# A two-block transformer forward pass on one core: GpSimd's modulation sums, the places of their tiles, shift and scale as rows, and the order of the memory attention

## The chip, the cores and the metric

One core of one Trainium2 chip runs the whole computation in one launch. The metric is the time of the device in microseconds. Three runs of the kernel before gave 1160.01, 1160.11 and 1162.4 us; the median is 1160.11 us. All data is float32.

## The reference

`first_block` takes x (256 tokens, width 1024), a context of 256 tokens and a vector c. Cut to what matters here:

```
sh1, sc1, g1, sh2, sc2, g2 = split(silu(c) @ w_ada + b_ada, 6)      # 1024 each
hc = rmsnorm(ctx) * (1 + csc1) + csh1 ;  hl = rmsnorm(x) * (1 + sc1) + sh1
# gated linear attention (4 heads) and retention (4 heads) of hl, with states from hc
x = x + g1 * merge(gla, ret)
x = x + g2 * hier_moe(rmsnorm(x) * (1 + sc2) + sh2)                  # 32 experts, top 2
```

`second_block` then adds a sparse attention mixer, an attention over 256 memory tokens (4 heads of 128: softmax(q k / sqrt(128)) v, then w_xo), and a feed-forward of width 4096 with squared relu.

## The kernel before, in words

Every weight matrix is cut into tiles of 1 MB ([128, 2048]) that lie in DRAM in the order of their use, the stream. SP loads them into a ring of six slots, `ring`; four of TensorE's results at a time lie in PSUM banks 0 to 3. `plan()` writes both orders out by hand: `SUMS` is the order of TensorE's results, each a name such as `rv1.3` or `gate4`, and `FREED` says for each tile of the stream which event frees its slot. SP's `load(t)` waits for the event of tile t-6 and issues the load, strictly in the order of the stream. A result is announced by `sum_ready`, and `fresh(name)` on TensorE waits, by `sum_taken`, until the result four places earlier has been copied out. The readers (ScalarE or VectorE) must take the results in the order of `SUMS`.

The projections of the mixer are `folded` products of a pair of tiles: seven block products with sums of the weights that VectorE forms in place (`weights_fold`, L2341 to L2348), after which `blocks_summed` (L2375 to L2402) puts the blocks together. The order is `gk`, `gv0`, `gv1`, four products `e`, `rk`, `rv0`, `rv1`, `rq`, then eight states `sg`, `sr`, and then eight rounds of gates: `fac0` to `fac7` with `gate0` to `gate7`. In the first four rounds ScalarE makes exponentials (`decays`), VectorE multiplies them with q and k (`gla_factors`, L2468 to L2474), and TensorE forms the scores from them (L1667).

The modulation (sh2, sc2, g1, g2) does not run on TensorE as a whole: 16 tiles of w_ada, called ada tiles, go through the same ring, and `ADA_BEHIND` says how many stand behind which pair or gate. GpSimd's `tile_weighted` multiplies the eight 256-column pieces of such a tile with one silu(c) per partition (L697) and adds the pieces up in three steps of 1024, 512 and 256 columns (L699 to L703). What is left is a sum over the 128 partitions. For tiles 0 to 7 (sh2 and sc2) TensorE does it in `columns_summed` (L1506) after `rq`: 16 products of a 128x128 block with a column of ones, so that the result lies in columns of 8, and ScalarE copies it to `mod2` (L907). The sums 0 to 7 lie where `qdec`, a table of decays, is loaded later; sums 8 to 11 lie over `rkc`, which is free once `ctxk_ready` has come to 8; tiles 12 to 15 wait for `fac3`. Broadcast rows of small parameters, `rows`, are loaded by GpSimd's queue ahead of its first tile (L686).

The memory attention (`query_exps`, `query_turned` on ScalarE, `query_weighted`, `out_copied` on VectorE): for each of four heads ScalarE forms the exponentials of the scores (L1330), VectorE divides them by their sum (L3182), TensorE transposes them (L2147), ScalarE copies the transposed ones out (L1340), TensorE multiplies them with v (L2156), and VectorE copies the result out (L3188). TensorE runs the transposes of head n ahead of the product of head n-1. Then it goes on with w_xo (L2168).

The diff touches `plan`, `program` with its blocks for the engines (the nested `tile_weighted`, `columns_summed`, `query_exps` and `query_turned` are in it), and `stream_of`.

## Time and profile before

| | us |
|---|---|
| median of three runs | 1160.11 |
| profiled execution | 1161.98 |
| its span, first to last instruction | 1160.2 |
| TensorE busy in it | 1118.5 |
| VectorE busy | 567.3 |
| ScalarE busy | 304.9 |
| GpSimd busy | 190.7 |

PE is TensorE's matmuls, DVE VectorE, ACT ScalarE, POOL GpSimd, SP the queue that issues the loads. In a timeline each row has the start and the length in us, the engine and the line of the kernel, the operation with its output and input by name, their shapes, and how many instructions are merged (x); in brackets how long the engine was idle before, and what ended that.
### The profile page before, as it was taken

To read this page: it belongs to the slowest core of one execution; us is meant where nothing else is said; L and a number is where in the kernel's file an instruction comes from. 1 tells how busy PE (TensorE), PEld (TensorE's weight loads), DVE (VectorE), ACT (ScalarE), POOL (GpSimd) and SP (SyncE) were. 2 spreads that over 40 slices of the span, in tenths; PEclk is the share of its full clock that TensorE was granted. 3 is DMA by queue.
4 is the path that set the end of the run, shared out by engine and by line. 5 is a ranking of instruction groups with operands and counts; after the bars stand their busy time and mean duration, and the time that the engine had idled before them with its cause. 6 is when DMAs were issued, how large, how long until landed. Compare 5 with 4: busy or idle time off the path is not lost.

```text
span 1160.2 us, 16672 instructions
## 1 busy us (share of the span) xinstructions
PE 1118.5 (96%) x6704; PEld 842.0 (73%) x6704; DVE 567.3 (49%) x1161; ACT 304.9 (26%) x708; POOL 190.7 (16%) x219
## 2 busy tenths in 40 slices
PE   7999999999999999999999999999888989999998
PEld 6789888898887888885555554478666849997443
DVE  1345345423676585532222222238886435677555
ACT  4360010015412302151111110253574241321000
POOL 0053665644670020000000000010000000000000
PEclk9999999999999999999999999999989989999999
DMA  9952232453444444568999999833300413544541
GB/s 377 392 214 109 109 146 109 166 233 145 146 167 159 178 150 183 197 255 335 423 426 425 426 425 425 363 123 133 122 1 20 180 55 110 185 179 182 182 145 38
DMA packets 35020, 241.92 MB, mean 209 GB/s; under 512 B 3978, under 2 KB 4234, under 8 KB 6524
## 3 DMA queue, kind: packets, MB, share of 16 engines
q1 hardware_dynamic: 33500, 234.46, 51.9%
q0 software_dynamic: 864, 4.16, 0.9%
q10 hardware_dynamic: 576, 2.18, 0.5%
q8 instruction: 56, 0.92, 0.3%
q14 instruction: 24, 0.20, 0.0%
HBM read 239.74 MB, written 1.05 MB: 208 GB/s over the span
## 4 chain that ended last, share of the span: by engine, by line
PE 85%; DVE 6%; ACT 3%; DMA 2%; issue 2%; SPq 1%; DVEq 0%; ACTq 0%
PE bank L1440 20%; PE bank L1437 11%; PE bank L1836 10%; PE bank L2191 8%; PE bank L1417 7%; PE bank L1863 5%; PE bank L1488 4%; PE bank L1793 3%; PE bank L1800 2%; DMA arena<-in_stream 2%; PE bank L1408 2%; PE bank L1639 1%; PE bank L2168 1%; PE bank L1693 1%; PE bank L1696 1%
## 5 line engine op out<-in xcount | busy, mean ns | idle before, releaser
L1440 PE MATMUL bank<-ring,arena 128*128 128x256 f32 x784 | 174.2, 379 | 1.6 <-ACT arena L1260 0.7
L1440 PEld LDWEIGHTS bank<-ring,arena 128*128 128x128 f32 x784 | 148.0, 190 | 22.3 <-ACT arena L1260 1.0
L697 POOL TENSOR_SCALAR ring<-ring,sc,consts 128x256 f32<-128x256 f32 x128 | 89.9, 716 | 108.2 <-DMA ring<-in_stream 83.5
L868 ACT ACTIVATE arena<-bank 128x256 f32<-128x256 f32 x90 | 32.4, 381 | 193.9 <-PE bank L1440 158.3
L1417 PE MATMUL bank<-ring,arena 128*128 128x256 f32 x320 | 71.0, 380 | 0.0
L1417 PEld LDWEIGHTS bank<-ring,arena 128*128 128x128 f32 x320 | 60.3, 190 | 9.3 <-issue 0.8
L1437 PE MATMUL bank<-arena,ring 128*128 128x128 f32 x528 | 63.0, 275 | 0.0
L1437 PEld LDWEIGHTS bank<-arena,ring 128*128 128x128 f32 x528 | 61.7, 192 | 0.5
L1836 PE MATMUL bank<-ring,arena 128*64 128x256 f32 x512 | 57.0, 381 | 0.0
L1417 PE MATMUL bank<-ring,hTl 128*128 128x256 f32 x256 | 56.6, 379 | 0.0
L1417 PEld LDWEIGHTS bank<-ring,hTl 128*128 128x128 f32 x256 | 48.3, 190 | 8.1 <-issue 1.9
L1836 PEld LDWEIGHTS bank<-ring,arena 128*64 128x64 f32 x512 | 36.0, 137 | 24.1 <-issue 6.7
L1488 PE MATMUL bank<-ring,arena 128*128 128x256 f32 x224 | 51.8, 386 | 1.7 <-ACT arena L766 0.8
L2776 DVE TENSOR_TENSOR arena<-arena,bank 128x256 f32<-128x256 f32 x16 | 6.7, 422 | 93.6 <-ACT arena L1082 93.6
L1437 PE MATMUL bank<-memkv,ring 128*128 128x128 f32 x448 | 52.3, 275 | 0.0
L1437 PEld LDWEIGHTS bank<-memkv,ring 128*128 128x128 f32 x448 | 51.2, 192 | 0.0
L2341 DVE TENSOR_TENSOR ring<-ring 128x1024 f32<-128x1024 f32 x24 | 29.6, 1235 | 43.2 <-PE bank L1440 32.8
L1488 PEld LDWEIGHTS bank<-ring,arena 128*128 128x128 f32 x224 | 42.5, 193 | 8.9 <-ACT arena L766 1.0
L1082 ACT ACTIVATE arena<-bank 128x256 f32<-128x256 f32 x16 | 6.1, 383 | 157.0 <-PE bank L1836 157.0
L741 POOL TENSOR_SCALAR arena<-arena,rA 128x1024 f32<-128x1024 f32 x2 | 5.7, 2830 | 252.7 <-ACT arena L1034 252.7
L1440 PE MATMUL bank<-ring,hTl 128*128 128x256 f32 x192 | 45.6, 380 | 0.0
L766 ACT ACTIVATE arena<-bank 128x512 f32<-128x512 f32 x38 | 22.2, 604 | 87.7 <-PE bank L1417 26.5
(514 smaller groups left out, 2012.5 us busy)
## 6 DMA issues: line engine op xcount, KB each, us to landing
ring<-in_stream SPq DMA_DIRECT2D x163, 1024.0 KB, 7.2
arena<-in_stream SPq DMA_DIRECT2D x38, 1024.0 KB, 13.4
hTl<-in_stream SPq DMA_DIRECT2D x9, 1024.0 KB, 11.7
hTc<-in_stream SPq DMA_DIRECT2D x9, 1024.0 KB, 13.6
consts<-in_consts ACTq DMA_DIRECT2D x1, 1408.0 KB, 12.9
arena<-in_mem SPq DMA_DIRECT2D x2, 512.0 KB, 5.2
arena<-in_x SPq DMA_DIRECT2D x1, 1024.0 KB, 18.8
arena<-in_ctx SPq DMA_DIRECT2D x1, 1024.0 KB, 23.4
```

Of the source, the lines that this page charges most:

```text
L697: pool.tensor_scalar(wk, wk, scv[:, k, 0:1], ones[:, 0:1], ALU.mult, ALU.mult).then_inc(ada_step, 1)
L868: ins = act.activation((p[:, 0, :], p[:, 1, :], first)[n], b, ACT.Copy)
L1408: mm = pe.matmul(b[:, 256 * n:256 * n + 256], w[:, k, 128 * n:128 * n + 128], h[:, k, :], start=(k == 0), stop=(k == KD - 1))
L1417: mm = pe.matmul(b[:, 256 * i:256 * i + 256], h[:, k, 128 * i:128 * i + 128], w[:, k, :], start=(k == 0), stop=(k == KD - 1))
L1437: mm = pe.matmul(b[:, 128 * n:128 * n + 128], rhs[:, k, 128 * n:128 * n + 128], lhs(*source, k), start=(start and k == 0 and n == 0), stop ...
L1440: mm = pe.matmul(b, lhs(*source, k), rhs[:, k, :], start=(start and k == 0), stop=(k == 3), skip_group_check=True)
L1488: mm = pe.matmul(b[:, 256 * i:256 * i + 256], h[:, k, 128 * i:128 * i + 128], w[:, k, :], start=(k == 0 and i == 0), stop=(k == KD - 1), s ...
L1793: mm = pe.matmul(gather_bank(o, k)[:, 256 * j:256 * j + 256], xn2[:, j, 128 * k:128 * k + 128], Pm[:, j, :], start=True, stop=True)
L1836: mm = pe.matmul(bank[0][CAP * e:CAP * e + CAP, FF * a:FF * a + FF], rows_k[:, at:at + CAP], w[e][:, k, :], start=(k == 0), stop=(k == KD ...
L1863: mm = pe.matmul(bank[1 + m][to:to + CT, :], hT_PT[n % 2][:, of:of + CT], wd[e][:, k, 512 * m:512 * m + 512], start=(k == 0), stop=(k == 1 ...
L2191: mm = pe.matmul(prod[m][:, :], lhs, rhs, start=(q == 0), stop=(q == 15))
L2341: dve.tensor_tensor(b11, b12, b11, ALU.subtract).then_inc(weights_folded, 1)
```

## The change

It has five parts. GpSimd adds the eight pieces of a tile in seven additions of 256 columns, each waiting for the one before. The ada tiles stand at other places of the stream: behind gk, gv0, gv1, rk, rv0, rv1, rq and gates 0 to 7 there were 1, 1, 2, 1, 2, 1, 1 and 1, 1, 1, 1, 1, 1, 1, 0 tiles, and now there are 1, 2, 2, 2, 2, 2, 1 and 0, 1, 1, 1, 1, 0, 0, 0. Shift and scale are summed as rows: a column of ones is the stationary operand, the sums of a tile are the 256 moving columns, and the four tiles of `sh` go to output partitions 0, 32, 64 and 96 of one bank, those of `sc` likewise, between `rv1` and `rq`; VectorE copies the eight rows into `rows`, which was cleared before, TensorE transposes them after `rq` into a new result, `mod2`, and ScalarE takes every 32nd column of it. The broadcast that fills `rows` is issued after that. GpSimd runs tiles 8 to 11 before it waits for the modulation and loads `qdec`. In the memory attention ScalarE makes the exponentials of all four heads first, and VectorE copies out the transposed ones of head 0 in its place.

```diff
@@ -143,9 +143,10 @@
 
 
 
-ADA_STEPS = KD + 3
+ADA_STEPS = KD + 7
 TURNS = (4, 5, 7, 8, 2, 0, 1, 3)
-ADA_BEHIND = {"gk": 1, "gv0": 1, "gv1": 2, "rk": 1, "rv0": 2, "rv1": 1, "rq": 1, "gate": 1}
+ADA_BEHIND = {"gk": 1, "gv0": 2, "gv1": 2, "rk": 2, "rv0": 2, "rv1": 2, "rq": 1, "gate": (0, 1, 1, 1, 1, 0, 0, 0)}
+ROWS_BEHIND = {"rv1": ("sh", "sc"), "rq": ("mod2",)}
 
 
 def plan():
@@ -191,16 +192,16 @@
     for name in ("rk", "rv0", "rv1", "rq"):
         pair(name)
         ada(ADA_BEHIND[name])
-    sums.extend(["sh", "sc"])
+        sums.extend(ROWS_BEHIND.get(name, ()))
     sums.extend(f"sg{h}" for h in range(HEADS))
     sums.extend(f"sr{h}" for h in range(HEADS))
     sums.append("fac0")
     tile("gate0")
-    ada(1)
+    ada(ADA_BEHIND["gate"][0])
     for i in range(7):
         sums.append(f"fac{i + 1}")
         tile(f"gate{i + 1}")
-        ada(ADA_BEHIND["gate"] * (i < 6))
+        ada(ADA_BEHIND["gate"][i + 1])
 
     pair("mg0")
     sums.extend(["g1a", "g1b"])
@@ -683,7 +684,8 @@
             pool.wait_ge(adaT_ready, 2)
             pool.dma_start(wr[:, :], wr_d).then_inc(small_in, 16)
             pool.dma_start(wukv[:, :], wukv_d).then_inc(small_in, 16)
-            pool.dma_start(rows[:, :], rowdram.partition_broadcast(P)).then_inc(rows_in, 16)
+            pool.wait_ge(cleared, 2)
+            pool.memset(rows[:, 0:2 * TC], 0.0).then_inc(cleared, 1)
             scv = sc[:, :].rearrange("p (k c) -> p k c", c=2)
             ada_at = [t for t, (kind, _) in enumerate(FREED) if kind == "ada"]
 
@@ -695,24 +697,27 @@
                 for k in range(KD):
                     wk = w[:, TC * k:TC * k + TC]
                     pool.tensor_scalar(wk, wk, scv[:, k, 0:1], ones[:, 0:1], ALU.mult, ALU.mult).then_inc(ada_step, 1)
-                pool.wait_ge(ada_step, ADA_STEPS * n + KD)
-                pool.tensor_tensor(w[:, 0:1024], w[:, 0:1024], w[:, 1024:2048], ALU.add).then_inc(ada_step, 1)
-                pool.wait_ge(ada_step, ADA_STEPS * n + KD + 1)
-                pool.tensor_tensor(w[:, 0:512], w[:, 0:512], w[:, 512:1024], ALU.add).then_inc(ada_step, 1)
-                pool.wait_ge(ada_step, ADA_STEPS * n + KD + 2)
-                pool.tensor_tensor(ada_sum(n), w[:, 0:256], w[:, 256:512], ALU.add).then_inc(ada_step, 1)
-
-            pool.wait_ge(cleared, 2)
+                wk = w.rearrange("p (k n) -> p k n", k=KD)
+                for k in range(4):
+                    pool.wait_ge(ada_step, ADA_STEPS * n + KD + k)
+                    pool.tensor_tensor(wk[:, k, :], wk[:, k, :], wk[:, k + 4, :], ALU.add).then_inc(ada_step, 1)
+                for k in range(2):
+                    pool.wait_ge(ada_step, ADA_STEPS * n + KD + k + 4)
+                    pool.tensor_tensor(wk[:, k, :], wk[:, k, :], wk[:, k + 2, :], ALU.add).then_inc(ada_step, 1)
+                pool.wait_ge(ada_step, ADA_STEPS * n + KD + 6)
+                pool.tensor_tensor(ada_sum(n), wk[:, 0, :], wk[:, 1, :], ALU.add).then_inc(ada_step, 1)
+
+            pool.wait_ge(cleared, 3)
             pool.wait_ge(sc_ready, 2)
             pool.wait_ge(consts_in, 32)
             for n in range(8):
                 tile_weighted(n)
             pool.wait_ge(ctxk_ready, 8)
-            tile_weighted(8)
-            pool.wait_ge(sum_ready, NO["sc"] + 1)
+            for n in range(8, 12):
+                tile_weighted(n)
+            pool.wait_ge(sum_ready, NO["mod2"] + 1)
             pool.dma_start(C("qdec"), cdram[:, where["qdec"][0]:where["kdec"][0]]).then_inc(qdec_in, 16)
-            for n in range(9, 12):
-                tile_weighted(n)
+            pool.dma_start(rows[:, :], rowdram.partition_broadcast(P)).then_inc(rows_in, 16)
             pool.wait_ge(sum_ready, NO["fac3"] + 1)
             for n in range(12, 16):
                 tile_weighted(n)
@@ -899,13 +904,17 @@
             folded("rk", [parts_l, parts_c], [head_block(rqk[:, :, 1, :])(0, 0), rkc[:, 0, 0:256]])
             for p in range(2):
                 folded(f"rv{p}", [parts_l, parts_c], [v[:, 0, 512 * p:512 * p + 256] for v in (rv, rvc)])
+            for _ in ("sh", "sc"):
+                taken.one()
             folded("rq", [parts_l], [head_block(rqk[:, :, 0, :])(0, 0)])
             act.wait_ge(sum_taken, taken.n)
-            act.wait_ge(sum_taken, NO["sh"])
-            for q, name in enumerate(("sh", "sc")):
-                b = take(name)
-                act.activation(mod2[:, KD * q:KD * q + KD], b[:, 0:KD], ACT.Copy).then_inc(sum_taken, 1)
-                taken.one()
+            b = take("mod2")
+            src = b[:, :].rearrange("p (s n g r) -> p s g n r", s=2, n=2, g=4)[:, :, :, :, 0]
+            dst = mod2[:, :].rearrange("p (s g n) -> p s g n", s=2, g=4)
+            for q in range(2):
+                act.activation(dst[:, q, :, :], src[:, q, :, :], ACT.Copy).then_inc((act_step, sum_taken)[q], 1)
+            step.one()
+            taken.one()
             for h in range(HEADS):
                 copy(f"sg{h}", sg[:, h, :, :])
             for h in range(HEADS):
@@ -1339,14 +1348,11 @@
                     act.wait_ge(av_done, 2 * STEPS + m - 1)
                 act.activation(xPT[m % 2], bank[(NO["xp00"] + 2 + m % 2) % NB][:, :], ACT.Copy).then_inc(pt_taken, 1)
 
-            query_exps(0)
-            query_exps(1)
-            query_turned(0)
-            query_exps(2)
-            query_turned(1)
-            query_exps(3)
-            query_turned(2)
-            query_turned(3)
+            for n in range(XH):
+                query_exps(n)
+            act.wait_ge(pt_taken, 2 * STEPS + 4 + 1)
+            for m in range(1, XH):
+                query_turned(m)
             preload(ACT.Sqrt)
             act.wait_ge(ox_ready, 4)
             preload(ACT.Sqrt)
@@ -1498,13 +1504,22 @@
                 return mm
 
             pe.wait_ge(tables_in, 16)
-            def columns_summed(name, at):
+            def shifts_summed(name, at):
 
                 b = fresh(name)
                 pe.wait_ge(ada_step, ADA_STEPS * (at + 4))
-                for k in range(KD):
-                    mm = pe.matmul(b[:, k:k + 1], ada_sum(at + k // 2)[:, 128 * (k % 2):128 * (k % 2) + 128], ones[:, 0:1],
+                for g in range(4):
+                    mm = pe.matmul(b[32 * g:32 * g + 1, 0:TC], ones[:, 0:1], ada_sum(at + g),
                                    start=True, stop=True, skip_group_check=True)
+                mm.then_inc(sum_ready, 1)
+
+            def shifts_turned():
+
+                pe.wait_ge(cleared, 3)
+                pe.wait_ge(sum_taken, NO["sc"] + 1)
+                b = fresh("mod2")
+                for blk in range(4):
+                    mm = pe.transpose(b[:, 128 * blk:128 * blk + 128], rows[:, 128 * blk:128 * blk + 128], ident)
                 mm.then_inc(sum_ready, 1)
 
             def rows_summed(name, at):
@@ -1626,10 +1641,11 @@
             for p in range(2):
                 folded(f"rv{p}", tile(), tile(), [latents, context])
                 pool_tiles(ADA_BEHIND[f"rv{p}"])
+            shifts_summed("sh", 0)
+            shifts_summed("sc", 4)
             folded("rq", tile(), tile(), [latents], features=True)
             pool_tiles(ADA_BEHIND["rq"])
-            columns_summed("sh", 0)
-            columns_summed("sc", 4)
+            shifts_turned()
             for name, kd, v, n in (("sg", kd_g, gvc, 4), ("sr", kd_r, rvc, 8)):
                 pe.wait_ge(ctxk_ready, n)
                 for h in range(HEADS):
@@ -1656,7 +1672,7 @@
 
             before_factors(0)
             token_rows("gate0", tile(), hl)
-            pool_tiles(ADA_BEHIND["gate"])
+            pool_tiles(ADA_BEHIND["gate"][0])
             for i in range(8):
                 f = fac[i % 2]
                 pe.wait_ge(factors, i + 1)
@@ -1682,7 +1698,7 @@
                 if i < 7:
                     before_factors(i + 1)
                     token_rows(f"gate{i + 1}", tile(), hl)
-                    pool_tiles(ADA_BEHIND["gate"] * (i < 6))
+                    pool_tiles(ADA_BEHIND["gate"][i + 1])
                 pe.wait_ge(scores_taken, i + 1)
                 if i >= 2:
                     pe.wait_ge(values_taken, i - 1)
@@ -2457,6 +2473,16 @@
                                       ALU.mult).then_inc(ctxk_ready, 1)
             for p in range(2):
                 folded(f"rv{p}", ring_tiles(PAIR_AT[f"rv{p}"]), [parts_l, parts_c], [block_of(rv, 512 * p), block_of(rvc, 512 * p)])
+            dve.wait_ge(cleared, 3)
+            for q, name in enumerate(("sh", "sc")):
+                dve.wait_ge(sum_taken, NO[name])
+                dve.wait_ge(sum_ready, NO[name] + 1)
+                for g in range(4):
+                    ins = dve.tensor_copy(rows[32 * g:32 * g + 1, TC * q:TC * q + TC], bank[NO[name] % NB][32 * g:32 * g + 1, 0:TC])
+                    if g < 3:
+                        S(ins)
+                        step.one()
+                ins.then_inc(sum_taken, 1)
             folded("rq", ring_tiles(PAIR_AT["rq"]), [parts_l], [head_block(rqk[:, :, 0, :])])
 
             def gla_factors(h):
@@ -3203,10 +3229,12 @@
             max_scaled(3)
             query_weighted(0)
             query_weighted(1)
+            dve.wait_ge(pt_ready, 2 * STEPS + 4 + 1)
+            dve.tensor_copy(xPT[0], bank[(NO["xp00"] + 2) % NB][:, :]).then_inc(pt_taken, 1)
+            query_weighted(2)
             out_copied(0)
-            query_weighted(2)
+            query_weighted(3)
             out_copied(1)
-            query_weighted(3)
             out_copied(2)
             out_copied(3)
             dve.wait_ge(sum_taken, NO["xp00"])
@@ -3328,7 +3356,7 @@
         s += [column_tile(win, at + 256 * j) for j in range(2)] + ada_tiles(ADA_BEHIND[name] if name else 0)
     gate_tiles = [column_tile(win, gga + 256 * i if i < 4 else rga + 256 * (i - 4)) for i in range(8)]
     for i in range(8):
-        s += [gate_tiles[i]] + ada_tiles(ADA_BEHIND["gate"] * (i < 7))
+        s += [gate_tiles[i]] + ada_tiles(ADA_BEHIND["gate"][i])
     for p in range(2):
         for w, at in ((win, mga), (win, mga + 1024), (a["w_branch_gla"][0], 0), (a["w_branch_ret"][0], 0)):
             s += [column_tile(w, at + 512 * p + 256 * j) for j in range(2)]
```

## Rows read from the trace of the kernel before

**Rows 1.** The page, part 1: busy time, share of the span, instructions.

```profile
PE 1118.5 (96%) x6704; PEld 842.0 (73%) x6704; DVE 567.3 (49%) x1161; ACT 304.9 (26%) x708; POOL 190.7 (16%) x219
```

**Rows 2.** Timeline of PE, 180 to 345 us: start, length, operation, idle before.

```profile
204.71 1.89 PE L1440 MATMUL bank<-ring,hTl 128*128 128x256 f32 x8
...
227.15 1.89 PE L1440 MATMUL bank<-ring,hTc 128*128 128x256 f32 x8
...
230.04 2.02 PE L1437 MATMUL bank<-hTl,ring 128*128 128x128 f32 x16 [1.00 <-DVE arena L2394]
...
242.62 3.63 PE L1506 MATMUL bank<-consts 128*128 128x1 f32 x32
...
246.12 15.75 PE L1639 MATMUL bank<-arena 128*128 128x256 f32 x64
...
271.18 0.49 PE L1667 MATMUL bank<-arena 128*128 128x128 f32 x2 [1.09 <-DVE arena L2474]
...
311.37 0.49 PE L1667 MATMUL bank<-arena 128*128 128x128 f32 x2 [0.90 <-DVE arena L2474]
...
325.75 7.07 PE L1417 MATMUL bank<-ring,hTl 128*128 128x256 f32 x32
```

**Rows 3.** Windows: busy time of each engine, PEclk (granted clock), DMA share.

```profile
240.00:256.00 16.00, 16.00 (x95) 14.51 (x95) 1.41 (x4) 2.74 (x6) 9.16 (x12) 0.89 0.66 263
...
930.00:945.00 15.00, 10.51 (x38) 6.64 (x38) 5.95 (x20) 8.32 (x23) 0.00 (x0) 0.77 0.00 1
```

**Rows 4.** Timeline of POOL, GpSimd's modulation tiles.

```profile
209.76 7.16 POOL L697 TENSOR_SCALAR ring<-ring,sc,consts 128x256 f32<-128x256 f32 x8 [12.44 <-DMA ring<-in_stream]
...
225.86 2.35 POOL L699 TENSOR_TENSOR ring<-ring 128x1024 f32<-128x1024 f32 x1
...
264.21 0.73 POOL L703 TENSOR_TENSOR arena<-ring 128x256 f32<-128x256 f32 x1
...
300.22 4.30 POOL L697 TENSOR_SCALAR ring<-ring,sc,consts 128x256 f32<-128x256 f32 x8 [24.65 <-PE bank L1652]
...
304.60 2.35 POOL L699 TENSOR_TENSOR ring<-ring 128x1024 f32<-128x1024 f32 x1
...
308.70 1.05 POOL L703 TENSOR_TENSOR arena<-ring 128x256 f32<-128x256 f32 x1
```

**Rows 5.** Timeline of DVE, 195 to 312 us.

```profile
202.25 0.76 DVE L2394 TENSOR_TENSOR arena<-arena 128x256 f32<-128x256 f32 x2
...
226.42 3.48 DVE L2394 TENSOR_TENSOR arena<-arena 128x256 f32<-128x256 f32 x2
...
267.56 2.27 DVE L2468 TENSOR_TENSOR arena<-arena 128x512 f32<-128x512 f32 x3 [24.31 <-ACT arena L944]
...
279.76 1.90 DVE L2468 TENSOR_TENSOR arena<-arena 128x512 f32<-128x512 f32 x3 [5.72 <-ACT arena L944]
...
305.78 4.53 DVE L2468 TENSOR_TENSOR arena<-arena 128x512 f32<-128x512 f32 x3 [5.03 <-ACT arena L944]
```

**Rows 6.** Timeline of PE, 30 to 62 us.

```profile
40.19 3.66 PE L1542 MATMUL bank<-arena 128*32 128x256 f32 x64 [0.51 <-DMA arena<-in_stream]
```

**Rows 7.** Timeline of all engines, 920 to 952 us, memory attention.

```profile
932.29 1.61 PE L2147 MATMUL bank<-consts,arena 128*128 128x128 f32 x8 [1.88 <-DVE arena L3182]
...
932.98 0.60 ACT L1340 ACTIVATE arena<-bank 128x512 f32<-128x512 f32 x1 [0.81 <-PE bank L2147]
...
933.47 0.56 ACT L1330 ACTIVATE arena<-bank,smx,qfac 128x256 f32<-128x256 f32 x1
...
935.74 0.43 DVE L3188 COPY arena<-bank 128x256 f32<-128x256 f32 x1 [2.72 <-PE bank L2156]
...
936.95 1.11 PE L2147 MATMUL bank<-consts,arena 128*128 128x128 f32 x4 [1.24 <-DVE arena L3182]
...
941.01 0.66 PE L2147 MATMUL bank<-consts,arena 128*128 128x128 f32 x4 [1.24 <-DVE arena L3182]
...
943.38 9.18 PE L2168 MATMUL bank<-ring,arena 128*128 128x512 f32 x21
```

## The prediction

> **What bounds the kernel now.** I read the page first: TensorE is busy 96% of the span, VectorE 49%, ScalarE 26%, GpSimd 16% [rows 1]. So a cut on another engine is worth only what TensorE waits for it, and the 42 us in which TensorE is not busy are most of what can be won by waiting less. Second, the timeline of TensorE: around the change it waits three times, 1.00 us before `rq` (at 229.0), 1.09 us at 270.1 and 0.90 us at 310.5, each time for VectorE [rows 2]. Third, the windows with the granted clock: a busy TensorE also loses time where its clock is at the lower of its two levels (1.2 instead of 2.4 GHz). Mean 0.89 over 240 to 256 us is 3.5 us at half speed (16 x 0.11 x 2), which costs 1.75 us; mean 0.77 over 930 to 945 is 6.9 us at half speed [rows 3]. These five places are what the change can touch; everything else should shift as it is.
>
> The times below are of the profiled execution, 1161.98 us with a span of 1160.2; it is 1.9 us above the median of 1160.11, so I subtract the sum from the median.
>
> **GpSimd's sums in pieces.** Before, a tile has 8 products and adds of 1024, 512 and 256 columns. A VectorE addition with two SBUF operands that starts under one of these adds is held until it ends, and then the two engines take turns: L2394, twice 0.4 us normally, took 3.48 us [rows 5] while the 2.35 us add ran from 225.86 [rows 4]; L2468's three took 4.53 us from 305.78, against 1.90 us undisturbed [rows 5], beside the adds begun at 304.60. Under the products the price is small: 2.27 us at 267.56 [rows 4, 5]. The Trainium skill ("SBUF — State Buffer", Who interferes with whom) has the rule: a VectorE instruction with two SBUF inputs and a GpSimd one that reads SBUF exclude each other for the whole instruction. The trace agrees; it also says that VectorE's new copies out of PSUM, one input each, stay free.
>
> The cost: seven pieces of 0.73 us [rows 4] with 0.08 us between are 5.7 us, against 4.5 for three adds (304.60 less the gaps): 1.1 us more per tile, 16 times, on an engine that is 16% busy. The gain for VectorE is not simply the ratio of lengths. A short chain wins: two additions wait at most two pieces. A long chain loses, because it meets one piece per instruction. At 305.78 seven VectorE instructions follow one another (three L2468, four small). I lay the pieces out from 304.60: the first addition waits until 306.14, the next two and the four small ones wait behind a piece each (0.73, stretched to 1.05 like the one at 308.70 where a long VectorE instruction goes first), and the last ends at 311.7 instead of 311.3. So the wait of 0.90 us grows by **0.4 us**. Bounds: -0.9 (the wait goes) to +1.5.
>
> **Places in the stream.** Tiles 0 to 11 now all lie ahead of the gates, so GpSimd is done with tile 11 at about 246 instead of 275, and the factors at 267.56 run undisturbed: 0.37 us on L2468, 0.3 us on the small ones behind. The wait at 270.1 falls from 1.09 to 0.44: **-0.65 us** (bounds -0.9 and 0).
> What it could cost is a late weight tile. Pairs take 24.2 us (204.7 to 228.9, [rows 2]); two tiles of GpSimd behind a pair take about 2 x 12 = 24 us, one landing 5 us after the slot falls free (209.76, [rows 4]). The ring's next pair needs those slots a whole pair later, so some 12 us of slack are left. The slimmest place is `gate5`: SP issues it behind tile 15's load, which waits for tile 12, and tile 12 waits for `fac3`. From 300.22 [rows 4] tile 12 takes 11 us, the two loads 8 us more: 319.3, while `gate5` is needed at 325.75 [rows 2]. 6.5 us of slack, no cost. The broadcast of `rows` leaves GpSimd's queue at 47 us and returns at about 246 beside `qdec`; their readers come 60 us later and more. Nothing. The memset of `rows` ends before tile 0 lands: nothing.
>
> **Shift and scale as rows.** Removed: 16 matmuls with one moving column, 3.5 us from 242.62 to 246.12. The low clock of this stretch lies right behind them: the 64 matmuls begun at 246.12 took 15.75 us, where the 0.216 us per record of its neighbours (eight in 1.89 less the tail) give 13.8 [rows 2, 3]. Added, before `rq`: two times four matmuls with one stationary column into four groups of 32 output partitions. The matmuls of L1542, which also go to four such groups, run side by side: 64 records in 3.66 us, 0.46 us for four logical products [rows 6]. I take 0.45 us for `sh` and for `sc`; one after the other they would be 1.73 us each (0.216 per record, [rows 2]). Added, after `rq`: four transposes, at most the 0.66 us of [rows 7], as a stream 0.45.
> A new wait comes with it. TensorE's first product of `rq` needs the bank of `sh`, which VectorE frees after its last two additions of `rv1` (done at 229.9) and four copies, each 0.35 to 0.43 us long [rows 7]: 231.4, TensorE goes on at 231.55 against 230.04 before. In that gap lie the 0.9 us of row sums and the old wait of 1.00, whose cause (L2394) now only touches GpSimd's products or small pieces. VectorE's copies for `sc` then end at 232.9, just before `rq`'s first part is ready at 233.3, so ScalarE and the weight folds behind them wait for nothing new. `rq` keeps its 12.6 us (244.15), the transposes end at 244.6, L1639 starts then instead of at 246.12: **-1.5 us** (bounds: -2.6, if the wait is nil; -0.3, if the row sums run one after another).
> The low clock behind 246.12 should not come, as the 3.5 us of one-column matmuls ahead of it are gone: **-1.7 us** (bounds: -1.75; 0, if the new idle time and one-row matmuls at 229 to 231.5 bring a fall of their own).
>
> **Memory attention.** Before, ScalarE has one order for exponentials and copies, so heads 2 and 3 start only at 933.47, after the copy that waited for the transposes (932.98) [rows 7]. TensorE then waits 1.24 us twice for VectorE's scaling, which in turn stands behind `out_copied` [rows 7]. After, ScalarE goes through all eight exponentials (a head is 1.1 us: done by 934.3), VectorE takes head 0's copy (0.7 us), scaling of head 2 is done at 934.55 instead of 936.9, of head 3 by about 936.1 instead of 941.0. TensorE has 4 x (0.45 + 0.86) us of work at the full clock from 932.29. Laid out event by event, with the clock low for 3.5 us from head 1's transposes on, as long as behind 246.12, and not for the 6.9 us of before [rows 3], the last product ends and L2168 starts at 939.7 instead of 943.38: **-3.7 us**. With a full clock throughout it would be 938.4 (-5.0), with the clock low as long as before 941.4 (-2.0). The 1.88 us wait ahead of 932.29 [rows 7] stays: nothing in front of it changes.
>
> **Sum.** 0.4 - 0.65 - 1.5 - 1.7 - 3.7 = -7.15 us: 1160.11 - 7.15 = **1153.0 us**.
>
> **The rivals.** (a) The clock falls where it did not: at 229 to 231.5 TensorE now idles 1.6 us beside 0.9 us of one-row matmuls. For it: before 932.29 an idle time of 1.88 us was followed by a fall. Against it: the 1.00 us at 229 was not. 3.5 us more at the lower level cost 1.7: 1154.7. (b) The low clock in the memory attention lasts its 6.9 us again, 1154.7: half of the instructions there are transposes. For it: it stayed low before although TensorE had work of both kinds there (the four transposes at 936.95 took 1.11 us, those at 941.01 0.66); against it: the idle gaps between the heads go [rows 3, 7]. The Trainium skill ("TensorE: Matmul & The Clock Gate", Part 4: PE-mode transpose) states that transposes do not count as activity for the clock; no run here isolates that. (c) Only one of the two halves pays, for instance because the row sums are serial and the new VectorE copies are slower: 1157.5 to 1158.5. (d) Slower: GpSimd becomes the bound of the ring. If taking turns with VectorE stretches all pieces and products, so that a tile takes 22 us at 300, `gate5` lands 4 us late, `gate6` another 7, and the sum is +4: 1164.3. It decides from 17.5 us per tile; for it speaks only that the longest tile before took 12 us and each gets 1.1 more; against it the 6.5 us of slack. (e) No fall of the clock at all in the memory attention: 1151.7.
>
> **How the numbers follow.** My forecast 50% (own range 1151 to 1155.5), (a) 12%, (b) 12%, (c) 12%, (d) 5%, (e) 9%. The range 1150 to 1158.3 holds all but (d), a part of (c) and a remainder for what I did not see. Under 0.2% (2.3 us) cannot be told from no change in this kernel: faster is below 1157.8. Faster 0.84, same 0.10, slower 0.06.
>
> **What would show it.** Right: PEclk 1.00 in 240 to 256; row-sum matmuls of 0.45 us per four; TensorE idle about 1.6 us ahead of `rq`, 0.4 at 270 and 1.3 at 310 (shifted by the gains before); L2168 3 to 5 us closer behind the first transposes of the attention; no wait of TensorE for a DMA of `ring`. Wrong: a DMA wait at a gate, a granted clock of half at 231, a tile of GpSimd over 17 us, or the waits at 270 and 310 unchanged.

## The result, and the profile after

The kernel after took 1154.94 us in the median (20 executions, 1152.3 to 1158.15), the kernel before beside it 1160.76 us (1157.8 to 1168.65). The ratio is 0.9937, 95% interval 0.992 to 0.9953: 0.6% faster. I had predicted 1153.0, range 1150 to 1158.3. The profiled execution took 1155.67 us with a span of 1153.9, against 1160.2 before; all differences below are of these two unless another is named. The page, part 1, of the kernel after:

```profile
PE 1114.2 (97%) x6692; PEld 838.0 (73%) x6692; DVE 564.5 (49%) x1170; ACT 304.2 (26%) x707; POOL 208.2 (18%) x284
```

GpSimd works 17.5 us more (16 tiles by 1.1) and nobody waits for it. TensorE around the change, timeline after, against [rows 2]:

```profile
229.68 1.04 PE L1512 MATMUL bank<-consts 128*1 128x256 f32 x16
...
232.55 2.02 PE L1443 MATMUL bank<-hTl,ring 128*128 128x128 f32 x16 [1.83 <-DVE rows L2481]
...
245.12 0.60 PE L1522 MATMUL bank<-consts,rows 128*128 128x128 f32 x4
...
245.56 13.98 PE L1655 MATMUL bank<-arena 128*128 128x256 f32 x64
...
268.00 0.49 PE L1683 MATMUL bank<-arena 128*128 128x128 f32 x2 [0.24 <-DVE arena L2500]
...
307.69 0.49 PE L1683 MATMUL bank<-arena 128*128 128x128 f32 x2 [0.40 <-DVE arena L2500]
```

Read from the top: all 16 records of the row sums in 1.04 us, so the four column groups run side by side; the wait ahead of `rq` at 1.83 us, where it was 1.00, now for VectorE's copies; the 64 products of the states in 13.98 us, where they took 15.75; the two waits for the gate factors at 0.24 and 0.40 us, where they were 1.09 and 0.90. VectorE's side of it, against [rows 5]:

```profile
227.12 1.55 DVE L2410 TENSOR_TENSOR arena<-arena 128x256 f32<-128x256 f32 x2
...
230.62 3.58 DVE L2481 COPY rows<-bank 1x256 f32<-1x256 f32 x8
...
265.24 1.90 DVE L2494 TENSOR_TENSOR arena<-arena 128x512 f32<-128x512 f32 x3 [19.49 <-ACT arena L953]
...
302.60 3.16 DVE L2494 TENSOR_TENSOR arena<-arena 128x512 f32<-128x512 f32 x3 [5.03 <-ACT arena L953]
305.69 0.81 DVE L2498 TENSOR_TENSOR arena<-arena 128x128 f32<-128x128 f32 x1
306.42 0.28 DVE L2500 TENSOR_TENSOR arena<-arena 128x128 f32<-128x128 f32 x1
306.63 0.81 DVE L2498 TENSOR_TENSOR arena<-arena 128x128 f32<-128x128 f32 x1
307.36 0.28 DVE L2500 TENSOR_TENSOR arena<-arena 128x128 f32<-128x128 f32 x1
```

and GpSimd's, against [rows 4]:

```profile
227.61 3.25 POOL L703 TENSOR_TENSOR ring<-ring 128x256 f32<-128x256 f32 x4
...
301.42 3.80 POOL L703 TENSOR_TENSOR ring<-ring 128x256 f32<-128x256 f32 x4
```

The memory attention, timeline after, against [rows 7], and the windows after, against [rows 3] (PEclk is the third number from the end):

```profile
930.89 1.45 PE L2163 MATMUL bank<-consts,arena 128*128 128x128 f32 x8 [1.88 <-DVE arena L3208]
...
932.82 0.62 ACT L1349 ACTIVATE arena<-bank 128x512 f32<-128x512 f32 x1
...
934.70 0.66 PE L2163 MATMUL bank<-consts,arena 128*128 128x128 f32 x4
...
937.07 10.46 PE L2184 MATMUL bank<-ring,arena 128*128 128x512 f32 x24
```

```profile
240.00:256.00 16.00, 16.00 (x101) 14.77 (x100) 2.91 (x7) 3.23 (x7) 8.99 (x14) 1.00 0.70 276
...
928.00:943.00 15.00, 12.99 (x51) 7.83 (x50) 7.78 (x25) 9.04 (x26) 0.00 (x0) 1.00 0.01 3
```

6.18 us from the first transposes (L2163) to w_xo (L2184) where there were 11.09; both waits of 1.24 us are gone and the clock stays at 2.4 GHz.

Where the 6.3 us of span came from, between the same instructions in both traces. Only the end of `rv1` is not the same instruction: before it is the end of its last product, after it is the start of the row sums, which comes 0.06 us earlier than that.

| stretch | before | after | difference |
|---|---|---|---|
| start to end of `rv1` | 229.04 | 229.68 | +0.64 |
| end of `rv1` to the states' products | 17.08 | 15.88 | -1.20 |
| states' products to `fac0` | 15.58 | 13.82 | -1.76 |
| `fac0` to the first scores | 9.48 | 8.62 | -0.86 |
| first to fourth scores | 40.19 | 39.69 | -0.50 |
| fourth scores to the wait at 777.11 / 773.14 | 465.74 | 465.45 | -0.29 |
| from there to the attention (untouched) | 155.18 | 157.75 | +2.57 |
| memory attention | 11.09 | 6.18 | -4.91 |
| w_xo to the end | 216.82 | 216.83 | 0 |

The loss of 2.57 us lies where the change edits nothing. One part of it is a gap of TensorE for which the profile shows no wait, in the kernel after:

```profile
801.14 5.08 PE L2003 MATMUL bank<-ring,arena 64*15 64x64 f32 x174
807.80 2.52 PE L2003 MATMUL bank<-ring,arena 64*15 64x64 f32 x82 [1.58 <-issue]
810.25 7.17 PE L1423 MATMUL bank<-ring,arena 128*128 128x256 f32 x32
```

Before, the same matmuls ran through:

```profile
805.10 7.32 PE L1987 MATMUL bank<-ring,arena 64*15 64x64 f32 x256
812.36 7.17 PE L1417 MATMUL bank<-ring,arena 128*128 128x256 f32 x32
```

From the first of them to the next product it is 9.11 us against 7.26, so the gap accounts for 1.85 us. The other 0.7 us lie behind it, where the clock is low for longer: 17.0 us in the whole stage against 13.6.

### The profile page after: what moved, and what is told of

Its sections match the earlier page's. It is cut to its first block, busy times and chain, and to the rows that moved or that the text cites. A ratio compares the mean times of both kernels' runs of the same rounds, so it can differ in the third digit from the quotient of the medians.

```text
span 1153.9 us, 16725 instructions
## 1 busy us (share of the span) xinstructions
PE 1114.2 (97%) x6692; PEld 838.0 (73%) x6692; DVE 564.5 (49%) x1170; ACT 304.2 (26%) x707; POOL 208.2 (18%) x284
## 4 chain that ended last, share of the span: by engine, by line
PE 87%; DVE 4%; ACT 4%; DMA 2%; issue 1%; SPq 1%; DVEq 0%; ACTq 0%
PE bank L1446 20%; PE bank L1443 11%; PE bank L1852 10%; PE bank L1423 8%; PE bank L2207 8%; PE bank L1879 5%; PE bank L1494 4%; PE bank L1809 3%; PE bank L1816 2%; DMA arena<-in_stream 2%; PE bank L1414 2%; PE bank L1655 1%; PE bank L2184 1%; PE bank L1709 1%; PE bank L1712 1%
## 5 line engine op out<-in xcount | busy, mean ns | idle before, releaser
L699 POOL TENSOR_SCALAR ring<-ring,sc,consts 128x256 f32<-128x256 f32 x128 | 94.1, 748 | 102.4 <-DMA ring<-in_stream 54.9
L703 POOL TENSOR_TENSOR ring<-ring 128x256 f32<-128x256 f32 x64 | 51.8, 810 | 5.1
```

What stands on the lines that cost most here:

```text
L699: pool.tensor_scalar(wk, wk, scv[:, k, 0:1], ones[:, 0:1], ALU.mult, ALU.mult).then_inc(ada_step, 1)
L703: pool.tensor_tensor(wk[:, k, :], wk[:, k, :], wk[:, k + 4, :], ALU.add).then_inc(ada_step, 1)
```

## The experiments

The table has one profiled execution of each kernel: TensorE's wait ahead of `rq` (for VectorE), the time from the states' products to `fac0`, its waits for the first and the fourth scores, the length of the memory attention, and how long the clock was low in 240 to 262 and in the attention (from windows of 10 us: length by (1 - PEclk) by 2). All in us.

| kernel | `rq` | to `fac0` | first | fourth | attention | low at 240 | low in it |
|---|---|---|---|---|---|---|---|
| before | 1.00 | 15.58 | 1.09 | 0.90 | 11.09 | 3.4 | 6.8 |
| before, again | 1.03 | 16.02 | 0.82 | 0.93 | 9.99 | 6.8 | 3.4 |
| attention only | 1.00 | 16.77 | 4.30 | 0.89 | 7.55 | 6.8 | 3.6 |
| columns of 64 | 1.00 | 13.87 | 0.68 | 0.89 | 9.99 | 0 | 3.4 |
| pieces only | 0 | 13.90 | 1.24 | 0.42 | 9.99 | 0 | 3.4 |
| places only | 0.95 | 16.40 | 0.25 | 0.93 | 12.35 | 6.8 | 10.2 |
| rows only | 2.00 | 13.82 | 0.80 | 0.92 | 8.85 | 0 | 0 |
| after | 1.83 | 13.82 | 0.24 | 0.40 | 6.18 | 0 | 0 |
| after, again | 1.83 | 13.81 | 0.24 | 0.40 | 6.18 | 0 | 0 |
| after, old attention | 1.83 | 13.81 | 0.24 | 0.41 | 9.99 | 0 | 3.4 |
| after, long additions | 2.00 | 13.82 | 0.25 | 0.91 | 6.18 | 3.4 at 234 | 0 |
| one bank | 0 | 13.81 | 0.25 | 0.42 | 7.42 | 0 | 3.6 |

In the three profiles with 6.8 us at 240 the clock fell while the last one-column products were still running: these took 4.84 us ("before, again"), 4.11 ("attention only") and 4.46 ("places only"), and 3.63 in the other two kernels that have them. So "to `fac0`" holds only a part of what the low clock cost there.

### The attention's order alone

The kernel before with the change's last part.

```diff
-            query_exps(0)
-            query_exps(1)
-            query_turned(0)
-            query_exps(2)
...
+            for n in range(XH):
+                query_exps(n)
+            act.wait_ge(pt_taken, 2 * STEPS + 4 + 1)
+            for m in range(1, XH):
+                query_turned(m)
...
+            dve.wait_ge(pt_ready, 2 * STEPS + 4 + 1)
+            dve.tensor_copy(xPT[0], bank[(NO["xp00"] + 2) % NB][:, :]).then_inc(pt_taken, 1)
...
```

> The kernel before with the new order of the memory attention alone (eight exponentials first, head 0's transposed copy on VectorE). Theory: the attention's part is independent of the rest; from the first transposes (L2147) to the first product of w_xo (L2168) it takes 6.2 us as in the changed kernel instead of 11.1, whether or not the front is changed, and the time falls by 4.9 us, about 0.4%. Rival 1: the full clock in this stretch came only from the front's shift by 4 us; alone, the clock is low for 3.5 us and the stretch takes 7.4 us (-3.7), or for 6.9 us and it takes 9.1 (-2.0). Rival 2: the gain is given back behind it, in w_xo or the feed-forward: the distance from L2168 to the end then exceeds the 216.8 us of both kernels.

1158.12 us (12 executions) against 1160.75, ratio 0.9976 (0.9953 to 0.9999). The attention took 7.55 us with 3.6 us at the low clock; for that case the prediction's layout has 7.4. So the order gives 3.5 us against the old order with 6.8 us low, but with as much low clock in both (9.99 us in "before, again") it gives 2.4, and with none in either (8.85 in "rows only", 6.18 after) 2.7. Rival 1 had the number (7.4 us with 3.5 us low), and the expected 4.9 us came to 2.6 in the median. Its reason, that only the front's shift keeps the clock up, is not borne out: "one bank" has the front and its shift, and 3.6 us low too. Rival 2 is out: from w_xo to the end it is 216.8 us again. The profiled execution was one of the long ones (1164.48), and its trace shows VectorE against GpSimd's long additions at their worst:

```profile
270.21 5.43 DVE L2465 TENSOR_TENSOR arena<-arena 128x512 f32<-128x512 f32 x3 [25.98 <-ACT arena L944]
```

```profile
270.76 2.66 POOL L699 TENSOR_TENSOR ring<-ring 128x1024 f32<-128x1024 f32 x1
273.50 1.59 POOL L701 TENSOR_TENSOR ring<-ring 128x512 f32<-128x512 f32 x1
```

```profile
277.03 0.56 PE L1664 MATMUL bank<-arena 128*128 128x128 f32 x2 [4.30 <-DVE arena L2471]
```

The low clock at 240 had lasted 6.8 us there, so `fac0` came 1.2 us further behind the states' products than in [rows 2], and VectorE met the additions, not the products ahead of them: the same program waited 4.30 us in place of 1.09.

### Everything but the attention's order

The kernel after with the attention of before (the diff above, reversed).

> The changed kernel with the old order of the memory attention: the front's three parts alone (pieces, places, rows). Theory: the front is worth 1.2 (row sums in the place of the column products) + 1.8 (no low clock behind them) + 0.9 (wait at 270) + 0.5 (wait at 311) = 4.3 us up to the last gate, so 0.35 to 0.4% if the granted clock in the sparse attention (775 to 930 us) is as before. Rival: the 2.6 us that this untouched stretch took longer in the changed kernel belong to the front's change and come again: then the whole is worth only 1.7 us, and the distance from the wait at 773 to the memory attention is 153.9 us again instead of 151.3.

1159.05 us, ratio 0.9972 (0.9951 to 0.9992). The front's waits are those of the kernel after to 0.02 us, the attention is back at 9.99. Up to the fourth scores the front gained the 4.3 us expected (78.04 us from the end of `rv1`, where there were 82.33), yet the median is only 1.7 us below the kernel before, which is what the rival had: the untouched stage took 156.56 us against 155.18, with a gap of 1.39 us at 808.0. So a part of that loss comes with the front's change. Each half pays; rival (c), that only one does, is out, though the upper ends of both intervals (0.9992 and 0.9999) lie just below 1.

### 64 moving columns in place of one

The kernel before, its 16 one-column products widened.

```diff
-                    mm = pe.matmul(b[:, k:k + 1], ada_sum(at + k // 2)[:, 128 * (k % 2):128 * (k % 2) + 128], ones[:, 0:1],
+                    mm = pe.matmul(b[:, 64 * k:64 * k + 64], ada_sum(at + k // 2)[:, 128 * (k % 2):128 * (k % 2) + 128], ones[:, 0:64],
```

> The kernel before, with each of the 16 one-column products of the modulation (L1506) fed with 64 columns of ones instead of one; ScalarE takes every 64th column. The weight loads (0.108 us per record) set the pace either way, so the products themselves should again take 3.5 us. Theory: it is the lack of moving columns in these 3.5 us that brings the low clock behind them; now PEclk stays 1.00 in 240 to 256 us, the states' products (L1639) take 13.8 instead of 15.6 us, and the kernel is 1.8 us faster (0.15%). Rival: the fall has another cause (the wait of 1.0 us at 229, or the weight-load-bound products as such): PEclk is again 0.89 over 240 to 256 and the time is unchanged.

1159.85 us, ratio 0.9981 (0.9962 to 0.9999). The products take as long as with one column (3.52 us against 3.50), and the clock does not fall behind them in the profile:

```profile
240.00:256.00 16.00, 16.00 (x103) 14.85 (x103) 1.51 (x4) 3.34 (x7) 9.00 (x12) 1.00 0.67 263
```

The median is 0.9 us below the kernel before, half of the 1.8 expected; in the profile 0.80 us went into the gap in the untouched stage.

### GpSimd's seven additions alone

The kernel before with the change's first part (`tile_weighted` and `ADA_STEPS` as in the diff above the prediction).

> The kernel before with one edit: GpSimd's sums in seven additions of 256 columns in place of three of 1024, 512 and 256. Theory of the prediction (a VectorE addition meets one piece per instruction, so a short chain gains and a long one loses): the wait before `rq` at 229 falls from 1.00 us to about 0, the three additions at 270 (L2464) keep about 4 us, because tile 11's work still lies beside them, the wait at 311 grows from 0.90 to about 1.3. Time -0.4 to 0 us. Rival, from the trace after (two small VectorE additions of 128 columns slip in beside each piece, 0.28 us each, and the three long ones take 3.16 us): the wait at 311 falls to 0.40, so -1.0 at 229, -0.5 at 311, between 0 and -0.6 at 270; 1.5 to 2.0 us less. The third case: the time does not move by more than its spread, because the low clock elsewhere takes it (ratio 0.998 to 1.001).

1157.71 us (12) against 1161.96, ratio 0.9948 (0.9927 to 0.9969): the edit that I had priced as a loss of 0.4 us is the largest gain of the parts run alone. It is more than the 1.5 to 2.0 us of the rival, for two reasons. None of its 12 executions took over 1163 us, where 16 of the 34 beside it of the kernel before did; against the other 18 (median 1160.1) it gains 2.4 us. And in its profile, 4.1 us shorter in span, 1.7 us are the low clock that did not come behind the one-column products and 1.1 us are in the attention, which it does not touch (9.99 us against 11.09). The waits alone gave 1.0 before `rq` and 0.5 at the fourth scores. By the ratios it even stands ahead of all three parts of the front together (0.9972); the intervals overlap, and in the traces the three parts reach the fourth scores 1.2 us sooner (307.71 against 308.94) and lose 2.0 us from there to the attention (622.39 us against 620.38). The wait ahead of `rq` is gone:

```profile
229.70 1.95 PE L1440 MATMUL bank<-hTl,ring 128*128 128x128 f32 x16
...
245.70 14.06 PE L1642 MATMUL bank<-arena 128*128 128x256 f32 x64
```

and the wait for the fourth scores is 0.42 us as in the kernel after. The clock did not fall behind the one-column products here, though they are unchanged. So those products do not lower it every time: in five profiles with them four had a low stretch there (3.4, 6.8, 6.8, 6.8 us) and this one had none; in nine with rows or with 64 columns none had a low stretch there. This profile is also the only one of the five in which TensorE had no idle time of about 1.0 us ahead of `rq` (0.95 to 1.03 in the four). Whether a fall needs the idle time and the one-column products together was not tested.

### The places alone

The kernel before with the new `ADA_BEHIND`, the loops that read it, and tiles 8 to 11 run together, as in the diff above the prediction.

```diff
-ADA_BEHIND = {"gk": 1, "gv0": 1, "gv1": 2, "rk": 1, "rv0": 2, "rv1": 1, "rq": 1, "gate": 1}
+ADA_BEHIND = {"gk": 1, "gv0": 2, "gv1": 2, "rk": 2, "rv0": 2, "rv1": 2, "rq": 1, "gate": (0, 1, 1, 1, 1, 0, 0, 0)}
```

> The kernel before with one edit: GpSimd's tiles 8 to 11 in the places of the change, all ahead of the gates, three long additions as before. Theory: the wait at 270 depends on tile 11's additions lying beside the three VectorE additions and nothing else, so it falls from 1.09 to 0.24 us; the wait at 311 stays at 0.9 (tile 12 still starts behind `fac3`); the wait at 229 stays near 1.0 or moves with GpSimd's phase (0 to 2.5 us). -0.85 us. It should also have none of the executions at 1165 us that the kernel before has, if these come from the collision at 270 in its long form (4.30 us seen once). Rival: those long executions come from the clock or the start-up and stay, with the same share as in the kernel before.

1161.56 us, ratio 0.998 (0.9958 to 1.0002). The wait for the first scores is 0.25, that for the fourth stays 0.93. That is -0.84 us at its place and not measurable in the whole. Two of 12 executions still took over 1163 us, the profiled one 1165.35, with a wait of 0.25 us in place of the long collision, so the collision at 270 is not the only thing that makes an execution long. Its clock was low for 6.8 us at 240 and 10.2 us in the attention:

```profile
240.00:262.00 22.00, 22.00 (x122) 19.98 (x121) 3.35 (x5) 3.82 (x8) 7.01 (x8) 0.84 0.58 235
932.00:950.00 18.00, 13.50 (x43) 8.66 (x42) 6.08 (x21) 8.45 (x24) 0.00 (x0) 0.72 0.00 1
```

### The kernel after with the long additions

```diff
-                for k in range(4):
-                    pool.wait_ge(ada_step, ADA_STEPS * n + KD + k)
-                    pool.tensor_tensor(wk[:, k, :], wk[:, k, :], wk[:, k + 4, :], ALU.add).then_inc(ada_step, 1)
...
+                pool.wait_ge(ada_step, ADA_STEPS * n + KD)
+                pool.tensor_tensor(w[:, 0:1024], w[:, 0:1024], w[:, 1024:2048], ALU.add).then_inc(ada_step, 1)
...
```

> The kernel after with one edit taken back: GpSimd's sums in three additions of 1024, 512 and 256 columns. Theory from the prediction's layout: wait at 311 0.9 in place of 0.40 us, wait at 268 stays 0.24, wait before `rq` 1.8 us or, if an addition of 1024 columns lies beside VectorE's additions of rv1, up to 2 us more. So 0.5 to 2.5 us slower than the kernel after: 1155.4 to 1157.4. Rival (pieces are worth nothing, places did it all): the same time as the kernel after, with the wait at 311 at 0.4.

1157.47 us, ratio 0.995 (0.993 to 0.9971). That is 0.13% slower than the kernel after by the ratios, and the two intervals overlap; in the trace it is clearer, 18.10 us from the row sums to the states' products against 15.88. The fourth scores wait 0.91 us again, and VectorE's two additions of `rv1` are held:

```profile
226.88 0.76 DVE L2402 TENSOR_TENSOR arena<-bank,arena 128x256 f32<-128x256 f32 x2 [1.91 <-PE bank L1443]
227.68 3.45 DVE L2407 TENSOR_TENSOR arena<-arena 128x256 f32<-128x256 f32 x2
```

With them comes what rival (a) had foreseen:

```profile
231.18 0.61 PE L1509 MATMUL bank<-consts 128*1 128x256 f32 x8 [0.34 <-DVE arena L2407]
233.79 3.54 PE L1440 MATMUL bank<-hTl,ring 128*128 128x128 f32 x16 [2.00 <-DVE rows L2478]
```

```profile
234.00:238.00 4.00, 4.00 (x24) 4.00 (x25) 1.99 (x5) 0.38 (x1) 2.58 (x5) 0.63 1.01 422
```

The clock falls to 1.2 GHz behind the idle time: 16 records take 3.54 us where they took 2.02. It did so in this one of the eight profiles whose row sums go ahead of `rq`; five of the others had an idle time of 1.8 to 2.0 us there, two had none, and all seven kept 2.4 GHz.

### The rows alone

The kernel before with shift and scale as rows, old places, long additions.

> The kernel before with one edit: shift and scale as rows in place of columns (the places of tiles 8 to 15 and the three long additions stay). Theory: eight moving columns of ones gone, the row sums' 16 records take about 1.05 us for both, VectorE's eight copies 0.45 us each, the wait inside `rq` about 1.8 us (up to 3.8 if GpSimd's 1024-column addition still lies beside VectorE there); from the end of rv1 to the states' products 15.9 us in place of 17.1; no low clock behind the states' products (13.8 us to fac0 in place of 15.6). Sum -3.0 us, less what the wait grows: 1157 to 1158.5. Rival: the low clock was not brought by the one-column matmuls but by the idle time ahead of them, and it comes again at 244 to 260: -1.2 us.

1160.34 us, ratio 0.998 (0.9958 to 1.0001). The end of `rv1` to the states' products took 16.65 us (before 17.08, after 15.88), and no low clock came behind. The expected 1157 to 1158.5 us was missed. So the rows alone give 0.43 us in their own stretch and need the pieces for the rest, because VectorE must be done with `rv1` before it copies: its two additions of `rv1` (L2411) took 3.52 us beside GpSimd's addition of 1024 columns, and the row sums themselves waited 0.41 us for them.

### One bank, four copies

The largest term left from the change is the wait of 1.83 us that it brought. Here `sh` goes to columns 0 to 255 and `sc` to 256 to 511 of one bank, and VectorE takes both in four copies.

```diff
-ROWS_BEHIND = {"rv1": ("sh", "sc"), "rq": ("mod2",)}
+ROWS_BEHIND = {"rv1": ("shsc",), "rq": ("mod2",)}
...
+                        mm = pe.matmul(b[32 * g:32 * g + 1, TC * q:TC * q + TC], ones[:, 0:1], ada_sum(4 * q + g),
...
-                    ins = dve.tensor_copy(rows[32 * g:32 * g + 1, TC * q:TC * q + TC], bank[NO[name] % NB][32 * g:32 * g + 1, 0:TC])
+                ins = dve.tensor_copy(rows[32 * g:32 * g + 1, 0:2 * TC], bank[NO["shsc"] % NB][32 * g:32 * g + 1, 0:2 * TC])
```

> The changed kernel with shift and scale summed into one PSUM bank and one place of the order, four copies of 512 columns in the place of eight of 256. Theory: TensorE's wait of 1.83 us before rq is the wait for the four copies out of sh's bank; with one place less, the first product of rq needs only rv1's bank and starts within 0.3 us of the row sums, so the wait shrinks by 1.5 to 1.8 us and the states' products start that much earlier. Price at risk: VectorE ends its copies at about 233.5 instead of 234.2 (4 x 0.7), but the weight folds of rq are then wanted 1.8 us earlier, so up to 1 us of the gain can come back as a wait inside rq. Rival: the wait is set by rv1's last additions on VectorE (done at 230.5): then the wait stays above 1 us. Total against the kernel before: about -8 us (0.68%), against the changed one -1.0 to -1.8.

1153.37 us (6 executions), ratio 0.9923 (0.9894 to 0.9953). The same kernel once more:

> The kernel after with shift and scale in one bank and four copies of 512 columns, once more, now with more executions beside the kernel before: 1152.5 to 1154.5 us, 1.0 to 1.8 us below the kernel after, no wait in `rq`, 14.0 us from the end of rv1 to the states' products. If the earlier 1153.37 was luck of six executions, it is at 1155.

1152.56 us (6), ratio 0.9925 (0.9903 to 0.9947). TensorE does not wait between the row sums and `rq`:

```profile
229.17 1.04 PE L1512 MATMUL bank<-consts 128*1 128x256 f32 x16
230.18 2.02 PE L1442 MATMUL bank<-hTl,ring 128*128 128x128 f32 x16
...
243.19 13.98 PE L1654 MATMUL bank<-arena 128*128 128x256 f32 x64
```

14.02 us from the row sums to the states' products (14.03 the first time), against 15.88: 1.85 us saved, twice. VectorE's four copies of 512 columns take 2.84 us where eight of 256 took 3.58. This version has the lowest median of all and beats the kernel before. The interval of its ratio overlaps that of the kernel after, so that it beats this one too, by the 1.85 us, rests on the traces.

### GpSimd made slower

Rival (d) put the point where GpSimd bounds the ring at 17.5 us per tile. The kernel after, with two multiplications by one more ahead of each product of tiles 12 to 15:

```diff
+SLOWER = 2
...
+                    for _ in range(SLOWER * (n >= 12)):
+                        pool.tensor_scalar(wk, wk, ones[:, 0:1], ones[:, 0:1], ALU.mult, ALU.mult).then_inc(cleared, 1)
+                        pool.wait_ge(cleared, 3 + extra.one())
```

> The kernel after with GpSimd made slower on its tiles 12 to 15: each of the eight products of a tile is preceded by two more multiplications by one, in place, so that a tile takes about 21 us in place of 12 (24 products of 0.75 us with their waits, seven additions). It tests rival (d), the slower case: that the ring is bound by GpSimd from 17.5 us per tile. Prediction's sum: `gate5` can be issued when tile 12 is done; 21 us from 297 is 318, the two loads behind it take 8 us, so it lands at 326 where TensorE wants it at 322: a wait of about 4 us for a DMA of `ring`, and others behind it at `gate6` and `gate7`; 1160 to 1164 us in all. The other side: if the loads have more slack than I counted, there is no DMA wait and the time is that of the kernel after within 1 us, and rival (d) was further away than 17.5 us per tile.

1185.85 us (4), ratio 1.0206 (1.0176 to 1.0236). Tile 12 took 23.9 us (296.50 to 320.44). TensorE at `gate5` and `gate6`, and later at the router:

```profile
327.68 9.94 PE L1429 MATMUL bank<-ring,hTl 128*128 128x256 f32 x32 [6.65 <-DMA ring<-in_stream]
...
349.10 9.47 PE L1429 MATMUL bank<-ring,hTl 128*128 128x256 f32 x32 [6.31 <-DMA ring<-in_stream]
...
410.56 3.60 PE L1737 MATMUL bank<-wr,mod 128*128 128x36 f32 x16 [8.10 <-DVE mod L2620]
```

If `gate5` lands earlier by as much as tile 12 is shorter, a tile 6.65 us shorter would not have been waited for: an estimate of 23.9 - 6.65 = 17.3 us per tile, where the prediction had 17.5. The mechanism of rival (d) is real, its place is `gate5` and `gate6` as said, and the kernel after stands 6 us away from it with its 11.2 us (297.05 to 308.21). Its price was too low: 1160 to 1164 us expected, 31 us above the kernel after measured. The load of the bias rows stands behind the tiles in GpSimd's queue (it was issued at 391.7), and VectorE waited 12.11 us for them ahead of L2616 and L2620, which gave the third wait, and the clock fell around the waits (58.0 us at the lower level in all, against 17.0).

### Second profiles of both kernels

> The kernel after, unchanged, for a second profile. Theory: what the kernel after lost in the stage 773 to 928 us (2.6 us, clock and one gap of 1.58 us at 807.8 in which TensorE waits for nothing the profile shows) varies from execution to execution and is no effect of the change; the waits at 232.5, 268.0, 307.7 and the row sums do not vary: 1.83, 0.24, 0.40, 1.04 us again within 0.05. Rival: the stage takes 153.9 us again with the same stretches at the lower clock, so it belongs to the kernel.

> The kernel before, unchanged, for a second profile. Waits 1.00, 1.09 and 0.90 us again if they are fixed by the program; the stage 777 to 928 us takes 151.3 us again if that is the kernel's own, 153 to 154 if not. If this execution is one of those near 1166 us, I expect the low clock behind the states' products for 6.8 us in place of 3.4 and a wait at 270 to 277 of about 4.3 us in place of 1.09, as in the run with the attention's order alone.

After: 1154.02 us, span 1152.2. All waits of the front are the same to 0.01 us, and so is the attention. The untouched stage took 156.39 us (157.75 in the first profile), low clock 13.6 us (17.0), gap at 807.2 of 1.29 us (1.58). Before: 1162.31, span 1160.5; the stage took 153.72 us (155.18), without the gap. This was not one of the executions near 1166 us, although its clock was low for 6.8 us at 240. Its waits were 1.03, 0.82 and 0.93 us, so the one for the first scores is not fixed by the program. So some 1.4 us of the stage vary from execution to execution in either kernel, and about 2.6 us separated the two kernels both times. The expectation that the loss is no effect of the change was wrong.

The gap accounts for 1.9 and 1.6 us of it, and in these 14 profiles it goes with the program, not with the time at which the stage is reached. It was absent in the three profiles "before", "before, again" and "attention only" (first of the 256 records at 805.1, 808.0 and 812.7), 0.80 to 0.84 us long behind record 162 with the pieces, the places or the 64 columns alone (802.4, 807.3, 803.1), and 1.29 to 1.75 us behind record 174 in all eight profiles with the row sums, also in the one with the slow GpSimd, which comes there at 835.0. The page's DMA queue `q8 instruction` moves a packet of 16 KB in this stretch in every profile. In the eleven with the gap the packet starts 3.1 to 4.3 us behind the first record, and TensorE goes on 2.3 to 2.6 us after the packet's start (kernel after: 805.2 and 807.8); in the three without it starts 1.1 to 2.2 us behind the first record. So the gap looks like a wait of TensorE for its own instructions. No run was made to test this, and what sets the place of the packet stays open.

## Why the prediction held, and where it was off

The time was 1.9 us above the forecast and inside its own range (1151 to 1155.5). That it came so near is in part luck, because two misses cancel. Between the two profiled executions the changed places gave 9.2 us where 7.15 were forecast, and everything else, which the prediction took to shift unchanged, cost 2.9 us. By its steps:

- **Pieces.** Predicted +0.4 us, measured -0.5 at the fourth scores: the one term with the wrong sign. My layout let each small addition wait behind a piece of its own. The rows after show two additions of 128 columns for each piece: L2498 0.81, L2500 0.28, then the same again. GpSimd's pieces, a narrow timeline of it:

```profile
306.43 0.86 POOL L706 TENSOR_TENSOR ring<-ring 128x256 f32<-128x256 f32 x1
307.36 0.85 POOL L708 TENSOR_TENSOR arena<-ring 128x256 f32<-128x256 f32 x1
```

L2500 starts at 306.42, just ahead of the piece at 306.43, which is then the one held (0.86 for 0.73); GpSimd needs 0.08 us between pieces, and that is where a second short addition goes in. The result lies inside the bounds of -0.9 and +1.5. "Pieces only" and "long additions" show 0.42 against 0.90 and 0.91. The further worth of the pieces at `rv1` (L2410 1.55 us where L2394 took 3.48) I had booked under the rows; without them the rows gain 0.4 in place of 1.2 us.
- **Places.** -0.65, measured -0.86. The first scores waited 0.24 us, not 0.44: with nothing beside them the three additions and the four small ones ran in 2.7 us. The wait before was longer by the 0.37 us on L2468 and by 0.28 and 0.20 us on two small additions, of which the prediction counted 0.3. "Places only" gives -0.84 alone.
- **Rows.** -1.5, measured -1.20. The row sums took 1.04 us (0.90 predicted); the eight copies took 0.45 us each (0.35 to 0.43 taken from rows of other shapes), and the wait came to 1.83 (1.6).
- **Low clock behind the columns.** -1.7, measured -1.76. Which edit removes it is less sure than I wrote: rows, 64 columns and the pieces alone each went without it. In the kernel before its length varied (3.4 us, then 6.8), so that the term met the number is also the luck of the profile it was read from.
- **Memory attention.** -3.7 with 3.5 us at the low clock, measured -4.91 with none, which is rival (e) at that place (6.18 us against the 6.1 laid out). With the low clock as assumed it took 7.41 to 7.55, against 7.4. Of the 4.91 us, 2.7 are the order at equal clock; the other 2.2 are low clock that one profile had and the other had not. Rival (b) was not seen with the new order: 0 to 3.6 us low in seven profiles, against 3.4 to 10.2 in six of the seven with the old one. In three of the seven the clock stayed at 2.4 GHz throughout, though half of the matrix instructions there are transposes.
- **Outside the change.** The prediction took everything else as shifting unchanged. The start cost 0.64 us more (0.02 in the second profile of the kernel after, 229.06: it varies), the stage after 773 us 2.57 more. These 3.2 us, less 0.3 in the stage ahead of it, against 2.1 us more gained than forecast at the changed places, leave the traces 0.8 us short of the forecast 7.15. The medians differ by 5.8 us, 1.3 short, and the median before was 0.65 us higher with 20 executions than the 1160.11 that I subtracted from. Together that is the 1.9 us. The step that failed is "everything else should shift as it is": the stage behind 773 us was 2.6 to 2.7 us longer in both pairs of profiles, 1.6 to 1.9 of it the gap.
- **Rival (a)** did not come in the kernel after, but did with long additions. **Rival (d)** is shown in its mechanism, its threshold is the estimate above. GpSimd's longest tile in the kernel after took 14.4 us (156.96 to 171.36); the prediction gave the longest before as 12 us, and it was 13.7 (155.92 to 169.60). Both lie ahead of the gates.

The Trainium skill ("SBUF — State Buffer", Who interferes with whom) adds that issue order, not shape, decides which engine blocks. The rows from 305.69 to 307.56 agree: the addition that starts ahead of GpSimd's piece takes 0.28 us, the one that starts under it 0.81.

## What to carry to other kernels

Where two engines exclude each other, lay out the start times on both sides, not only the lengths: a short piece is met once and lets a pair of short instructions through. Before a wait for copies is accepted, put the results side by side in one bank, so that fewer and longer copies release it. A change can cost or give as much in a stretch that it does not edit, by the clock and by gaps like the one at 807.8, as at its own place: compare the untouched stages too, and in several profiles.
